# Dilated attention beside a projection: the dilated groups by residue, the band by blocks, with an exchange of log sums

## What is computed

```python
DIL_PAIRS = ((128, 1), (512, 4), (2048, 16))

def _dilated_window_branch(q, k, v, span, dilation):
    L, W = T // dilation, span // dilation
    ...                                     # query and keys are put in residues of the position modulo dilation
    k_band = jnp.concatenate([prev(kb), kb], axis=4)
    s = jnp.einsum('bhrnqd,bhrnkd->bhrnqk', qb, k_band).astype(f32) * (Dh ** -0.5)
    dist = W + qi - kj
    mask = (dist >= 0) & (dist <= W) & ((blk > 0) | (kj >= W))
    s = jnp.where(mask, s, NEG_INF)
    lse = jax.nn.logsumexp(s, axis=-1)
    p = jnp.exp(s - lse[..., None])
    o = jnp.einsum('bhrnqk,bhrnkd->bhrnqd', p, v_band)
    ...

def _dilated_mixer(x, w_in, w_out, pos):
    z = x @ w_in                            # 3 x 1024 query columns, 1024 keys, 1024 values
    ...                                     # rotary on the first 32 of 128 channels of q and k
    for g, (span, dilation) in enumerate(DIL_PAIRS):
        o, l = _dilated_window_branch(q[:, g], k, v, span, dilation)
    wts = jax.nn.softmax(jnp.stack(lses, axis=0), axis=0)
    o = jnp.einsum('gbht,gbhtd->bhtd', wts, jnp.stack(outs, axis=0))
    return o @ w_out
```

## Time and profile before

| | us |
|---|---|
| median of 3 runs | 2455.95 (2452.67 to 2461.14) |
| the profiled execution | 2453.33 |
| its span in the trace | 2451.5 |
| TensorE busy in it | 2226.3 (91%) |
| VectorE busy | 1245.2 (51%) |
| ScalarE busy | 823.0 (34%) |

### The profile page before, as it was taken

The page is one execution under the profiler, slowest core; times in us unless marked ns, Lnnn a source line. Parts: engine busy times, 40 slices in busy tenths (PEclk is TensorE's granted clock), DMA queues, the critical chain, the costliest instruction groups (busy, mean ns, idle before and its releaser), DMA issues. The chain is left out here.

```text
span 2451.5 us, 32633 instructions
## 1 busy us (share of the span) xinstructions
PE 2226.3 (91%) x13452; PEld 1747.4 (71%) x13452; DVE 1245.2 (51%) x1679; ACT 823.0 (34%) x1256; POOL 317.2 (13%) x302
## 2 busy tenths in 40 slices
PE   8995886899999979999989999989996668999997
PEld 6862884678887767878768788876664446878875
DVE  4644762563243365555464454466676535543543
ACT  3335322353232243333243322352224234322222
POOL 0000000200000200000030690052441103000002
PEclk9998898899999989999999999999998669999998
DMA  5310000223232311212123223322110011323322
GB/s 201 95 43 13 2 4 1 95 86 95 95 95 86 95 61 61 70 61 69 36 69 112 91 95 97 101 86 95 52 43 5 1 69 63 118 77 113 96 76 70
DMA packets 50613, 177.22 MB, mean 72 GB/s; under 512 B 5617, under 2 KB 5617, under 8 KB 50209
## 3 DMA queue, kind: packets, MB, share of 16 engines
q1 hardware_dynamic: 46944, 164.65, 20.8%
q10 hardware_dynamic: 3168, 7.60, 0.8%
q0 software_dynamic: 352, 2.88, 0.3%
HBM read 170.92 MB, written 4.19 MB: 71 GB/s over the span
## 5 line engine op out<-in xcount | busy, mean ns | idle before, releaser
L859 DVE TENSOR_TENSOR w_lo<-w_raw,w_hi 128x1024 fp32r<-128x1024 f32 (+1 forms) x320 | 396.6, 1241 | 822.8 <-ACT w_hi L852 821.5
L852 ACT ACTIVATE w_hi<-w_raw 128x1024 fp32r<-128x1024 f32 (+1 forms) x320 | 329.1, 1031 | 890.2 <-PE banks L955 830.9
L953 PE MATMUL banks<-xh,w_hi 128*128 128x512 f32 x1560 | 620.7, 398 | 4.6 <-PEq L212 3.6
L955 PE MATMUL banks<-xh,w_lo 128*128 128x512 f32 x1560 | 609.8, 391 | 0.0
L954 PE MATMUL banks<-xl,w_hi 128*128 128x512 f32 x1560 | 609.1, 390 | 0.0
L953 PEld LDWEIGHTS banks<-xh,w_hi 128*128 128x128 f32 x1560 | 294.4, 189 | 81.6 <-issue 16.1
L955 PEld LDWEIGHTS banks<-xh,w_lo 128*128 128x128 f32 x1560 | 293.7, 188 | 62.8
L954 PEld LDWEIGHTS banks<-xl,w_hi 128*128 128x128 f32 x1560 | 294.3, 189 | 58.7 <-issue 0.7
L953 PE MATMUL banks<-hh,w_hi 128*128 128x512 f32 x688 | 270.2, 393 | 11.7 <-DVE w_lo L859 4.8
L955 PE MATMUL banks<-hh,w_lo 128*128 128x512 f32 x688 | 269.1, 391 | 0.0
L954 PE MATMUL banks<-hl,w_hi 128*128 128x512 f32 x688 | 268.9, 391 | 0.0
(11 more groups left out here) (495 smaller groups left out, 2932.1 us busy)
## 6 DMA issues: line engine op xcount, KB each, us to landing
w_raw<-in_w SPq DMA_DIRECT2D x128, 512.0 KB, 3.4
w_raw<-in_w_gu SPq DMA_DIRECT2D x44, 512.0 KB, 3.5
w_raw<-in_w_c_in SPq DMA_DIRECT2D x40, 512.0 KB, 3.4
w_raw<-in_w_ab_in SPq DMA_DIRECT2D x27, 512.0 KB, 3.5
w_raw<-in_w_in SPq DMA_DIRECT2D x25, 512.0 KB, 3.4
w_raw<-in_w_down SPq DMA_DIRECT2D x16, 384.0 KB, 3.1
w_raw<-in_w_down SPq DMA_DIRECT2D x16, 320.0 KB, 2.8
w_raw<-in_w_ab_out SPq DMA_DIRECT2D x8, 512.0 KB, 3.5
```

The source lines that it names most:

```text
L852: act.activation(core.w_hi[u % SLOTS][:, 0:n], core.raw[u % RAW][:, 0:n], ACT.Copy).then_inc(core.hi_ready, 1)
L859: dve.tensor_tensor(lo[:, 0:n], core.raw[u % RAW][:, 0:n], hi[:, 0:n].bitcast(F32), ALU.subtract).then_inc(core.split_ready, 1)
L953: pe.matmul(bank, hi[:, w], src.xh[:, kk, :], start=kk == 0, stop=False)
L955: mm = pe.matmul(bank, lo[:, w], src.xh[:, kk, :], start=False, stop=last)
```

## The change

A head is no longer worked through in four items of 128 neighbouring queries. Its band is scored by blocks as before, two blocks to a step, but the groups 1 and 2 are scored by residue: all 128 queries of a residue modulo 4 at once, by the 128 keys of the residue. The row maxima, exponentials and their sums are then taken apart for 8 row sets of a head: 4 blocks of the band (columns 0 to 3 of the small tiles) and 4 residues (columns 4 to 7).

- `score` has four steps r: blocks 0 and 1, blocks 2 and 3, residues 0 and 1, residues 2 and 3. They use the banks 3 and 7 in turn. One matmul of 256 columns adds the masks of each half.
- A query's band sum and its residue sum stand in other rows and columns. ScalarE takes the logarithm of the 8 sums, VectorE subtracts the negated maxima, spreads them over 32 columns each by a product with `eye32` (128 x 256), and TensorE moves them to the other order with two matmuls of 4 columns (`exchange`). VectorE adds the maxima, ScalarE takes the exponential, VectorE adds the own sums, takes the reciprocal, and scales the band (128 x 128 and 128 x 768) and the residues (128 x 512).
- `turn` has three steps of 3, 4 and 4 transposes; `mix` has three, with 3, 4 and 4 matmuls of 128 columns.
- The steps of a head, counted from j0: scores at 0 to 3 in `pe`; `values` of half 0 at 4 in `pe` and of half 1 at 5 in `middle`, now both through bank 5; `exchange` at 4 in `middle`; `turn` at 5, 6, 7; `mix` at 6, 7, 8; the result at 8. A head's steps now reach to step 8, with the next head's scores among them.
- The last steps are 40 to 47, still among the first three units of the next product, two of them behind its first slice and one behind each of the next six.
- Queries of the groups 1 and 2 are laid by residue over all 512 tokens. The masks are laid out anew, `eye32` and `quarter` are new constants, and the probabilities have their own tiles, two of each kind.

```diff
+    def score(self, pe, h, r):
+        ...
+        for e in range(2):
+            if r < 2:
+                qb = 2 * r + e
+                query, first = self.tile(h, 0)[:, qb * P:(qb + 1) * P], max(0, qb - 1)
+                cols = out[:, 2 * e * P:(2 * e + qb + 1 - first) * P]
+                pe.matmul(cols, query, key[:, first * P:(qb + 1) * P], start=True, stop=False)
+                mm = pe.matmul(cols, identb, both[0] if qb else core.mask("causal4"), start=False, stop=True)
+            else:
+                c = 2 * (r - 2) + e
+                keys = key.rearrange("p (j c) -> p c j", c=4)[:, c, :]
+                for g in range(2):
+                    pe.matmul(out[:, (2 * e + g) * P:(2 * e + g + 1) * P], self.tile(h, 1 + g)[:, c * P:(c + 1) * P], keys, start=g == 0, stop=False)
+                mm = pe.matmul(out[:, 2 * e * P:(2 * e + 2) * P], identb, both[1], start=False, stop=True)
+        mm.then_inc(s.scored, 1)
+    def exchange(self, pe, h):
+        pe.wait_ge(s.spread, h + 1)
+        ...
+        pe.matmul(core.psum[4][:, 4:8], flat[:, 0:P], quarter, start=True, stop=True)
+        pe.matmul(core.psum[4][:, 0:4], flat[:, P:2 * P], quarter, start=True, stop=True).then_inc(s.exchanged, 1)
     def pe(self, pe, j):
-        if (j - self.FROM) % 5 == 1 and self.item(j):
-            self.values(pe, self.item(j)[1])
-        if self.item(j - 1):
-            self.turn(pe, *self.item(j - 1))
-        if self.item(j):
-            self.score(pe, *self.item(j))
+        for h, n in self.heads_at(j, (5, 6, 7)):
+            self.turn(pe, h, n)
+        for h, r in self.heads_at(j, (0, 1, 2, 3)):
+            self.score(pe, h, r)
+        for h, _ in self.heads_at(j, (4,)):
+            self.values(pe, h, 0)
     def middle(self, pe, j):
-        if self.item(j - 2):
-            self.mix(pe, *self.item(j - 2))
+        for h, _ in self.heads_at(j, (4,)):
+            self.exchange(pe, h)
+        for h, _ in self.heads_at(j, (5,)):
+            self.values(pe, h, 1)
+        for h, n in self.heads_at(j, (6, 7, 8)):
+            self.mix(pe, h, n)
     def act(self, act, j):
+        for h, _ in self.heads_at(j, (4,)):
+            act.wait_ge(s.shifted, h + 1)
+            act.activation(other, other, ACT.Exp).then_inc(s.other, 1)
+        for h, half in self.heads_at(j, (4, 5)):
+            act.wait_ge(s.vturned, 2 * h + half + 1)
+            ...
+            act.activation(to, core.psum[5].rearrange("p (b k) -> p b k", k=P), ACT.Copy).then_inc(s.vtok_out, 1)
+        ...
+            if r == 3:
+                act.wait_ge(s.expd, 4 * h + 4)
+                act.activation(self.stat(h, "lse"), self.stat(h, "sum"), ACT.Ln).then_inc(s.logged, 1)
```

More of the change, by code:

```diff
@@ L868, in act @@
             for side, steps in part.ahead:
-                for j in steps:
+                for j in sum(steps, ()):
                     side.act(act, j)
@@ L994, in outer @@
                 if k < len(steps):
-                    side.pe(pe, steps[k])
+                    side.pe(pe, steps[k][0])
+                    for j in steps[k][1:]:
+                        side.middle(pe, j)
+                        side.pe(pe, j)
     def run(self, st, pool=None, sync=None, scalar_first=None, scalar_last=None):
@@ L2237, in __init__ @@
+        self.res = [st.placed(f"res{i}", [P, 2 * T], spare + (2 + 2 * i) * TILE) for i in range(2)]
         self.tiles = HeadTiles(ring, self)
-        self.s = st.sems("vturned vtok_out scored negmax expd inverted added prob_ready turned turned_out mixed src_hi src_lo", "dil_")
+        self.s = st.sems("vturned vtok_out scored negmax expd logged lse spread exchanged shifted other total inverted summed scaled "
+                         "turned turned_out mixed src_hi src_lo", "dil_")
         self.src_hi, self.src_lo = self.s.src_hi, self.s.src_lo
-    def item(self, j):
-        h, qb = divmod(j - self.FROM, 5)
-        return (4 * h + qb, h, qb) if 0 <= h < self.N_HEADS and qb < NT else None
@@ L2290, in turn, with stat @@
[L2290 to L2300 removed]
+    def stat(self, h, kind):
+        at = self.STATS + 8 * ("negmax", "sum", "lse", "other", "factor").index(kind)
+        return self.band[h % 2][:, at:at + 8]
@@ new lines, in values @@
+    def values(self, pe, h, half):
+        core, s, v = self.core, self.s, self.tile(h, 4)
+        if half == 0:
+            core.wait_left(pe, self.b0 + 5 * h + 4)
+        if 2 * h + half:
+            pe.wait_ge(s.vtok_out, 2 * h + half)
+        residue = v.rearrange("p (j c) -> p c j", c=4)
+        for b in range(NT):
+            src = residue[:, b, :] if half else v[:, b * P:(b + 1) * P]
+            mm = pe.transpose(core.psum[5][:, b * P:(b + 1) * P], src, core.const("ident"))
+        mm.then_inc(s.vturned, 1)
```

245 lines of the change are left out of this document (128 added, 117 removed).

## The result

| | before | after |
|---|---|---|
| median, us | 2458.55 (2452.67 to 2463.76, 4 runs) | 2506.69 (2505.56 to 2508.5, 4 runs) |
| profiled execution | 2453.33 | 2506.71 |
| its span | 2451.5 | 2504.9 |
| stage with the side work, first scores to the end of the last unit that holds some | 326.3 | 374.6 |

The changed kernel takes 1.0197 of the time before (95% interval 1.0171 to 1.0223), 48 us more. The forecast was 32 us more, 2475 to 2497 us by itself and 2463 to 2513 us with its first two rivals. The stage alone grew by 48.3 us. The other 5 us by which the two profiled spans differ lie outside it, 1.5 ahead of it and 3.6 behind. The code there is unchanged, and the cause stays open.

What follows compares the result with a forecast made beforehand. TensorE, always busy, bounds the kernel. Saved work, two new waits and clock loss in seven heads, plus the last head: -34 + 7 x (4.7 + 2.75 + 1.7) + 1.8 = +32 us, 2486 us; range 2475 to 2497, with two rivals 2463 to 2513.

Steps and rivals of the forecast that it cites:

- its first two rivals: Short waits with clock at 2.4 GHz, about 2468 us, chance 0.15; clock falls or long waits, about 2505 us, chance 0.11.
- spread ready, after S: VectorE's spread for the exchange, ready 8.65 us after S, the start of the side work behind a unit.
- exchange wait: TensorE at the exchange, half a unit behind the last scores, waits 4.7 us (4.2 to 5.4) for VectorE's spread.
- clock behind the exchange: Granted clock drops after TensorE's wait at the exchange, losing 1.7 us each time (0 to 2.8).
- TensorE back at the values after their first half: ScalarE's copy frees bank 5 for the second half of the values at S + 6.05 us.
- values' wait: TensorE, at the second half of the values, waits 2.75 us (2.3 to 3.3) for ScalarE's copy out of bank 5.
- clock behind the values' wait: No clock loss taken, as 2.75 us lay nearer to the 2.16 us idle time followed by clock 1.00.
- side work on TensorE: A changed head's transposes, scores, masks, mixing and exchange take 9.2 us for 13.5, saving 34 us over 8 heads.
- last head, both waits: Last head, among the next product's slices without VectorE's rotary: 1.4 us wait plus up to 0.5, about 1.8 us.
- the second rival: Clock falls behind both waits, or they are at their long ends: +60 us at most, about 2505 us; chance 0.11.
- a period above 48 us: Sign in the head's period: another wait in turning and mixing, or the clock falling twice in a head; forecast near 46.5.
- Two f32 matmuls of 128 columns take 0.44 us: TensorE price for f32 matmuls, within the changed head's nine 128-column score matmuls (2.0 us) and 11 mixing matmuls (2.4 us).

Runs made afterwards that it cites:

- e1_copyfirst: Changed kernel with ScalarE's copy of the values moved ahead of the exponential of the exchanged sums; 2479.4 us, 1.0089 of before.
- e2_early: Changed kernel with a head's last row maximum up to the spread moved ahead of the rotary on VectorE; 2466.5 us, 1.0034 of before.
- e3_both: Changed kernel with e1_copyfirst and e2_early together, and VectorE's addition behind the exchange ahead of the rotary too; 2447.1 us, 0.9953 of before.
- e4_contig: Changed kernel with residue keys read as 128 neighbouring columns, not every fourth (wrong keys, same work); 2504.2 us, 1.0179 of before.
- e5_contig_before: Kernel before the change with residue keys read as neighbouring columns, not every fourth (wrong keys, same work); 2449.4 us, 0.9969 of before.
- e6_fill: Changed kernel with 15 useless bf16 mask matmuls ahead of the exchange in TensorE's queue; 2492.7 us, 1.0144 of before.
- e10_top_first: e9_copy_later with VectorE's last row maximum up to the spread, and the addition behind the exchange, also ahead of the weight split; 2437.2 us, 0.9894 of before.
- e8_keys_copied: e3_both with VectorE's sum of dilated parts behind the band's scaling, plus GpSimd copying keys into residue order; 2442.3 us, 0.9939 of before.
- e9_copy_later: e8_keys_copied with GpSimd's key copy waiting until the head before is scaled; 2440.3 us, 0.9915 of before.

## Why the prediction held, and where its terms were off

Side by side, per head, with the profile after for the head of 974 to 998 us:

| step | predicted, us | measured, us |
|---|---|---|
| spread ready, after S | 8.65 | 982.57 - 974.11 = 8.5 |
| exchange wait | 4.7 | 3.5 |
| clock behind the exchange | 1.7 | 1.5 |
| TensorE back at the values after their first half | 6.05 | 993.42 - 987.42 = 6.00 |
| values' wait | 2.75 | 2.6 |
| clock behind the values' wait | 0 | 1.6 |
| side work on TensorE | 9.2 | 10.8 |
| last head, both waits | 1.8 | 1.35 + 0.46 = 1.8 |

The 1.5 us of clock behind the exchange are those of this one head. Over the seven heads they average 1.9 us, because the first and the fifth lose more.

**How much of it was luck.** The direction and the mechanism held, and the time lies in the stated range. It lies outside the forecast's own 2475 to 2497 us, and near the 2505 us of the second rival, whose clock falls behind both waits. The prediction's sign for that, a period above 48 us, came too (48.45). That the sum missed by 16 us and not by more is owed to two errors of opposite sign, the work and the exchange's wait.

**What held.** Both waits stand where they were put, with the releasers named, seven times each and a shorter one in the last head; the times of VectorE and ScalarE behind them are right within 0.2 us (the pieces of the 8.65 us add up to 8.73). `e1_copyfirst` and `e2_early` remove one wait each by its cause alone, and `e3_both` shows that nothing else makes the kernel slower.

**The step that failed, the work.** "Two f32 matmuls of 128 columns take 0.44 us" was taken from the mix, whose operands lie side by side, and used for the residue scores, whose keys lie four f32 apart. There a pair takes 0.89. Eight of them cost 1.8 us a head more; with 10.8 us from the period (48.45 less 8 half units at 2.84, the slow two at 4.38 and 4.43, and the waits of 3.5 and 2.6), the change saves 2.7 us a head on TensorE and not 4.3, 22 us over 8 heads and not 34. `e4_contig` shows the cause. The prediction had no row of a full matmul with such keys. The packed set in the earlier trace rows reads its keys in the same step, but that row doesn't show the step's price apart from the packing.

**The same error in the comparison.** I set 0.57 us for four matmuls of 32 queries against one full matmul at 0.22 us and took the row as speaking against the packing. With the same number of keys and the same stride, a full matmul takes 0.44, so a packed set is 0.13 us dearer and not 0.35. An estimate of what the packing brings takes an unpacked matmul of 32 queries at the price of a full one, which no run shows: four would take 1.78 us for the 0.57 of the packed set, 3.1 times; side by side it is four times 0.22, 0.88 us, against 0.36 (`e5_contig_before`), 2.4 times. The Trainium skill (TensorEngine Tiling (Array Packing), Theoretical Speedup) gives up to four times for column tiling by 32. The estimate doesn't reach four, but the page is nearer than my reading of the row.

**The first wait was oversized for the same reason.** The slower scores bring TensorE to the exchange 2 x 0.45 = 0.9 us later. With the spread 0.15 us early as well, it waits 3.5 us and not 4.7. A wait behind work that another engine determines takes back whatever the work is shortened or lengthened by; `e4_contig` shows the same with the other sign. The errors of work and wait thus partly cancel: the work alone would have put the result 8 x 1.6 = 13 us higher, the exchange's wait 7 x 1.2 = 8 us lower.

**The step that failed, the clock.** "Nothing for the other" wait rested on an idle time of 2.16 us behind which the clock is 1.00. Here the waits of 2.3 to 2.6 us had the clock at 0.52 to 0.65 behind them in all seven heads, 7 x 1.6 = 11 us: the fall behind both waits that the second rival (chance 0.11) named. It is, beside the 13 us of the work, the largest term that the sum missed. One row at 1.00 was no proof: in `e2_early` and in `e6_fill` the same wait of 2.6 us, with no long one ahead of it, is followed by a fall in four of seven heads and by none in three. So a wait of this length may or may not bring the clock down. Whether the wait of 3.5 us ahead of it is what made the fall so regular in the changed kernel, seven of seven against eight of fourteen, stays open; no run set the two at another distance. In `e4_contig`, with waits of 4.4 to 6.1 us ahead, it falls in six of seven heads, and not behind the first head's 2.27 us. The waits of 1.35 us and less left the clock at 1.00 in the changed kernel, `e2_early` and `e6_fill`, but even that is no rule. In the last head of `e10_top_first`:

```profile
1186.83 0.39 PE L2332 MATMUL banks<-consts,line 128*128 128x4 f32 x2 [1.35 <-DVE line L2455]
...
1189.00:1191.00 2.00, 2.00 (x7) 1.61 (x6) 0.87 (x4) 0.70 (x2) 0.00 (x0) 0.50 0.00 0
```

**The sum with the measured terms.** -8 x 2.7 + 25.2 (exchange waits of heads 0 to 6) + 17.8 + 7 x (1.5 + 1.6) + 1.8 = 45 us. Of the stage's 48.3, 3 us are not in it. 2.6 of them are the first and the fifth head: the exchange itself takes 0.88 us there and not 0.47, and the half unit behind it 5.26 and not 4.38. The first head's wait is longer, 4.2 us; the fifth's, 3.50, is like the others'.

## What to carry to other kernels

When work is taken from the engine that bounds, look first for what it will meet sooner: its queue mates on the other engines keep their order, so a result that is computed behind a rotary or behind another head's exponential becomes the bound, and moving a few short operations ahead in their queues (here -60 us with the clock) was worth more than the work saved (22). Price an instruction from a row with the same access pattern, not only the same shape. And put a price on the clock behind recurring waits like these, of 2.3 us and more, here about 1.6 us a time, even when one such gap in the trace had none. To see what one edit does, compare the stage that it touches before the whole time.

## What the runs showed of the hardware

- An f32 matmul of 128 columns whose moving operand is read in steps of four f32 takes 0.44 us, against 0.22 side by side (`e4_contig`; the pairs 0.89 and 0.44).
- The clock's fall behind a gap of 2.6 us is not settled by the gap and the work beside it: the same step gave 1.00 and 0.57 in two heads of one execution (`e2_early`). Of the last heads' waits of 1.35 us one had a fall to 0.50 behind it (`e10_top_first`), those of the changed kernel and `e2_early` none. Filling the longer wait with 15 useless matmuls, 3.2 us, made the kernel 14 us faster, the stage 16 (`e6_fill`).
- A copy of 128 x 512 f32 on GpSimd, 1.10 us, held a VectorE TENSOR_SCALAR of 128 x 128 f32 from 0.29 to 0.89 us (`e8_keys_copied`); moved away, it was 0.29 again (`e9_copy_later`). There the copy at 983.97 takes 1.93 us. It starts during VectorE's 1.22 us for `w_lo`, which begins at 983.74, and ends at 985.90, about 1 us behind it. That the copy was held in turn is likely, not tested.
- Four-column f32 matmuls cost little: the exchange takes 983.04 - 982.57 = 0.47 us for four records.
